# Eleven of 64 pairs of expert units multiplied with seven block products in place of eight, with the block sums made by VectorE

## The reference

```
q = (hb @ w_q) ; s = q . sub_keys ; top-k ; g = softmax(scores of the chosen experts)
act = gelu(einsum('bchkd,bcd->bchk', u[eidx], hb))
...
out = sum over the chosen experts of g * act * v[eidx]
```

## Time and profile before

| | |
|---|---|
| median of 3 timed runs | 2427.67 us (2426.92 to 2431.57) |
| span of the profiled execution, first to last instruction | 2425.6 us |
| TensorE busy | 2404.8 us, 99% |
| VectorE busy | 1756.2 us, 72% |
| ScalarE busy | 1399.6 us, 58% |
| GpSimd busy | 791.8 us, 33% |
| second expert product, layers 0 and 1 | from 867 to 1215 us and from 2073 to 2422 us |

### The profile page before, as it was taken

The page is one execution under the profiler, slowest core; times in us unless marked ns, Lnnn a source line. Parts: engine busy times, 40 slices in busy tenths (PEclk is TensorE's granted clock), DMA queues, the critical chain, the costliest instruction groups (busy, mean ns, idle before and its releaser), DMA issues.

```text
span 2425.6 us, 43553 instructions
## 1 busy us (share of the span) xinstructions
PE 2404.8 (99%) x17531; PEld 2231.4 (92%) x17531; DVE 1756.2 (72%) x2966; ACT 1399.6 (58%) x2071; POOL 791.8 (33%) x452
## 2 busy tenths in 40 slices
PE   9999999999999999999999999999999999999999
PEld 8999999999999988888898999999999999888887
DVE  7988787498489965555678886865974899655555
ACT  5586664444677754445555965644446777544444
POOL 0011410288898820000000113003888998100000
PEclk9999999999999999999999999999999999999999
DMA  6633345355544455566555333453555444555555
GB/s 255 220 122 123 107 144 193 137 186 183 176 163 159 157 187 195 191 215 234 180 191 208 120 126 109 154 186 135 184 183 174 161 162 157 191 191 192 196 194 173
DMA packets 96678, 419.24 MB, mean 173 GB/s; under 512 B 10848, under 2 KB 11360, under 8 KB 79584
## 3 DMA queue, kind: packets, MB, share of 16 engines
q1 hardware_dynamic: 96480, 416.47, 50.5%
HBM read 415.38 MB, written 1.05 MB: 172 GB/s over the span
## 4 chain that ended last, share of the span: by engine, by line
PE 90%; DVE 4%; ACT 2%; DMA 2%; issue 1%; POOL 1%; SPq 0%; DVEq 0%; ACTq 0%
PE banks L2179 28%; PE banks L389 18%; PE banks L391 18%; PE banks L390 18%; PE banks L2161 3%; DMA xr<-in_xstream 1%; PE banks L832 1%; DVE ring_lo L364 1%; PE banks L793 1%; PE banks L809 1%; DMA ring<-in_wstream 1%; POOL xr_lo L1838 1%; PE banks L849 1%; PE banks L2020 0%; PE banks L732 0%
## 5 line engine op out<-in xcount | busy, mean ns | idle before, releaser
L1833 ACT ACTIVATE xr_hi<-xr 128x1024 fp32r<-128x1024 f32 x512 | 541.2, 1058 | 537.1 <-DMA xr<-in_xstream 537.0
L1838 POOL TENSOR_TENSOR xr_lo<-xr,xr_hi 128x1024 fp32r<-128x1024 f32 x256 | 620.1, 2426 | 389.1 <-ACT xr_hi L1833 388.3
L389 PE MATMUL banks<-featH,xr_hi 128*128 128x256 f32 x2048 | 576.7, 282 | 1.8 <-POOL xr_lo L1838 1.8
L390 PE MATMUL banks<-featL,xr_hi 128*128 128x256 f32 x2048 | 575.7, 281 | 0.0
L391 PE MATMUL banks<-featH,xr_lo 128*128 128x256 f32 x2048 | 575.5, 281 | 0.0
L1838 DVE TENSOR_TENSOR xr_lo<-xr,xr_hi 128x1024 fp32r<-128x1024 f32 x256 | 313.8, 1226 | 297.9 <-ACT xr_hi L1833 297.7
L389 PEld LDWEIGHTS banks<-featH,xr_hi 128*128 128x128 f32 x2048 | 386.1, 189 | 2.6 <-POOL xr_lo L1838 1.8
L390 PEld LDWEIGHTS banks<-featL,xr_hi 128*128 128x128 f32 x2048 | 386.4, 189 | 0.0
L391 PEld LDWEIGHTS banks<-featH,xr_lo 128*128 128x128 f32 x2048 | 386.4, 189 | 0.0
L389 PE MATMUL banks<-featH,ring_hi 128*128 128x256 f32 x1232 | 351.8, 286 | 1.2 <-DVE ring_lo L364 0.8
L390 PE MATMUL banks<-featL,ring_hi 128*128 128x256 f32 x1232 | 346.3, 281 | 0.0
(11 more groups left out here) (372 smaller groups left out, 4141.9 us busy)
## 6 DMA issues: line engine op xcount, KB each, us to landing
xr<-in_xstream SPq DMA_DIRECT2D x512, 512.0 KB, 3.3
ring<-in_wstream SPq DMA_DIRECT2D x128, 1024.0 KB, 4.8
smw<-in_small SPq DMA_DIRECT2D x4, 617.0 KB, 10.1
...
big<-in_mix_row SPq DMA_DIRECT2D x4, 256.0 KB, 5.5
```

Source lines behind the costliest of these rows:

```text
L389: PE.matmul(o, s_hi_lo[0], m_hi_lo[0], start=first, stop=False)
L390: PE.matmul(o, s_hi_lo[0], m_hi_lo[1], start=False, stop=False)
L1833: A.activation(xr_hi[:, m % XR], xr[:, m % XR], ACT.Copy).then_inc(s_xhi, 1)
L1838: (PO if m < NKEY else V).tensor_tensor(xr_lo[:, m % XR], xr[:, m % XR], xr_hi[:, m % XR].bitcast(F32), ALU.subtract).then_inc(s_xlo_pool ...
```

## The change

Two units together are a product of a 2x2 block matrix of activations (two token halves by two units) with a 2x2 block matrix of weights (two units by two column halves): eight block products. For the 11 pairs in `SEVEN` the kernel now forms them with Strassen's scheme in Winograd's form: seven block products of four sums of activation blocks and four sums of weight blocks. Each block product has its three passes, so 21 matmuls take the place of 24. Three of the seven go to banks 0 to 2 directly, four gather in banks 4 to 7 over the 11 pairs and are added to x by VectorE at the end (`seven_sums`).

The 22 units of these pairs no longer pass through the ring. `PLAIN` lists the other 106, and `SEVEN_AT` the place in that list ahead of which a pair's seven products stand: 14, 26, 38, 46, then every 6 up to 88. The weights of such a pair come by four transfers of 256 KB (`b_load`) into one of two sets of own buffers: set 0 for pairs 1, 2, 3, 5, 7, 9, 11, set 1 for pairs 4, 6, 8, 10. The memory of set 1 is that of activations which the first 38 units have used up. ScalarE makes the high parts (3584 columns of weights and sums, 1024 of activations and sums), VectorE the sums and the low parts. The positions of these steps in the two engines' loops are tables: for a pair whose products stand ahead of place AT, the steps lie at AT-7 to AT-2, the last of them (`a_low`) at AT-2. The transfers and splits for layer 1's first weights are moved later, since they use buffers that the change needs. Unused semaphores are dropped.

```diff
+SEVEN = (7, 14, 21, 26, 30, 34, 38, 42, 46, 50, 54)
+SEVEN_SET = (0, 0, 0, 1, 0, 1, 0, 1, 0, 1, 0)
+PLAIN = tuple(i for i in range(NKEY) if i // 2 not in SEVEN)
+ONE_BY_ONE = len(PLAIN)
+SEVEN_AT = tuple(2 * r - 2 * j for j, r in enumerate(SEVEN))
...
+                b_sum = [alias(f"b_sum_{i}", [P, 4, 512], F32, offset=sums_at[i]) for i in range(2)]
+                b_sum_lo = [alias(f"b_sum_lo_{i}", [P, 4, 512], F32R, offset=sums_at[i]) for i in range(2)]
...
+                SHARED = tuple(j == 0 or SEVEN_SET[j] == SEVEN_SET[j - 1] or SEVEN_SET[j] not in SEVEN_SET[:j] for j in range(NS))
+                B_HIGH = tuple(SEVEN_AT[j] - 7 if SHARED[j] else SEVEN_AT[j - 1] - 1 for j in range(NS))
...
+                LAST_SUMS = tuple(SEVEN_AT[j] - 6 if SHARED[j] else SEVEN_AT[j - 1] - 1 for j in range(NS))
...
+                A_HIGH = tuple(SEVEN_AT[j] - 5 for j in range(NS))
...
+                SUMS_LOW = tuple(SEVEN_AT[j] - (3 if SHARED[j] else 4) for j in range(NS))
+                A_LOW = tuple(SEVEN_AT[j] - 2 for j in range(NS))
...
+                def load_after(j):
+                    if j == 0:
+                        return 1
+                    if SEVEN_SET[j] not in SEVEN_SET[:j]:
+                        return SEVEN_AT[j - 1]
+                    return max(SEVEN_AT[i] for i in range(j) if SEVEN_SET[i] == SEVEN_SET[j]) + 1
+                def set_free(j):
+                    return j if SHARED[j] and j else max(j - 1, 0)
...
+                    def b_load(j, piece):
+                        sp.wait_ge(s_xu, past(s_xu) + VU + load_after(j) + piece)
+                        if set_free(j):
+                            sp.wait_ge(s_bmul, past(s_bmul) + set_free(j))
+                        unit = VU + 2 * SEVEN[j] + piece // 2
+                        sp.dma_start(b_raw[SEVEN_SET[j]][:, piece],
+                                     xstream[layer * (2 * NKEY) + unit, :, 512 * (piece % 2):512 * (piece % 2 + 1)]
+                                     ).then_inc(s_bl[SEVEN_SET[j]], 16)
...
+                    def seven(j):
+                        b, unit = SEVEN_SET[j], 2 * SEVEN[j]
+                        q, c = unit // QUARTER, unit % QUARTER
+                        a = [(a_hi[b][:, 2 * n + t, :], acts_lo[q][:, c + n, t * P:(t + 1) * P]) for n, t in ((0, 0), (1, 0), (1, 1))]
+                        sums = [(a_sum_hi[b][:, n, :], a_sum_lo[b][:, n, :]) for n in range(4)]
+                        w11, w21, w22 = [(b_hi[b][:, n, :], b_lo[b][:, at, :]) for n, at in enumerate((0, 2, 3))]
+                        t1, t3, t2, t4 = [(b_hi[b][:, 3 + n, :], b_sum_lo[b][:, n, :]) for n in range(4)]
+                        pe.wait_ge(s_bmade, past(s_bmade) + 3 * j + 3)
+                        for p, w, o in ((a[0], w11, 4), (a[1], w21, 0), (sums[3], w22, 1), (a[2], t4, 2),
+                                        (sums[0], t1, 5), (sums[1], t2, 6), (sums[2], t3, 7)):
+                            PE.matmul(bank[o][:], p[0], w[0], start=o >= 4 and j == 0, stop=False)
+                            PE.matmul(bank[o][:], p[0], w[1], start=False, stop=False)
+                            mm = PE.matmul(bank[o][:], p[1], w[0], start=False, stop=o >= 4 and j == NS - 1)
+                        mm.then_inc(s_bmul, 1)
...
-                    for i in range(NKEY - TAIL, NKEY):
+                    for i in range(ONE_BY_ONE - TAIL, ONE_BY_ONE):
                         mm = value(i, 0)
                     mm.then_inc(s_vsum, 1)
-                    for i in range(NKEY - TAIL, NKEY):
...
+                    def b_high(j):
+                        b = SEVEN_SET[j]
+                        act.wait_ge(s_bl[b], past(s_bl[b]) + 64 * (SEVEN_SET[:j].count(b) + 1))
+                        A.activation(b_hi[b][:, 0, :], b_raw[b][:, 0, :], ACT.Copy)
+                        A.activation(b_hi[b][:, 1:3, :], b_raw[b][:, 2:4, :], ACT.Copy).then_inc(s_bhi, 1)
+                    def sums_high(j):
+                        b = SEVEN_SET[j]
+                        act.wait_ge(s_bmade, past(s_bmade) + 3 * j + 1)
+                        A.activation(b_hi[b][:, 3:7, :], b_sum[b][:], ACT.Copy).then_inc(s_bhi, 1)
+                    def a_high(j):
+                        if j == 0:
+                            act.wait_ge(s_xu, past(s_xu) + VU + 6)
+                        b, unit = SEVEN_SET[j], 2 * SEVEN[j]
+                        A.activation(a_hi[b][:].rearrange("p (i t) s -> p i (t s)", i=2), acts[:, unit:unit + 2, :], ACT.Copy
+                                     ).then_inc(s_bhi, 1)
+                    def a_sums_high(j):
+                        b = SEVEN_SET[j]
+                        act.wait_ge(s_bmade, past(s_bmade) + 3 * j + 2)
+                        A.activation(a_sum_hi[b][:], a_sum[b][:], ACT.Copy).then_inc(s_bhi, 1)
 
                     act.wait_ge(s_gev, past(s_gev) + GT)
...
+                        for j in range(NS):
+                            if i == B_HIGH[j]:
+                                b_high(j)
+                            if i == SUMS_HIGH[j]:
+                                sums_high(j)
+                            if i == A_HIGH[j]:
+                                a_high(j)
+                            if i == A_SUMS_HIGH[j]:
+                                a_sums_high(j)
...
+                    def first_sums(j):
+                        b = SEVEN_SET[j]
+                        w = b_raw[b]
+                        dve.wait_ge(s_bl[b], past(s_bl[b]) + 64 * (SEVEN_SET[:j].count(b) + 1))
+                        dch.link(V.tensor_tensor(b_sum[b][:, 0:2, :], w[:, 1:4:2, :], w[:, 0:2, :], ALU.subtract))
+                    def last_sums(j):
+                        b = SEVEN_SET[j]
+                        w, t = b_raw[b], b_sum[b]
+                        dch.link(V.tensor_tensor(t[:, 2, :], w[:, 3, :], t[:, 0, :], ALU.subtract))
+                        V.tensor_tensor(t[:, 3, :], w[:, 2, :], t[:, 2, :], ALU.subtract).then_inc(s_bmade, 1)
+                    def b_low(j):
+                        b = SEVEN_SET[j]
+                        dve.wait_ge(s_bhi, past(s_bhi) + 4 * j + 1)
+                        dve.wait_ge(s_bmade, past(s_bmade) + 3 * j + 1)
+                        V.tensor_tensor(b_lo[b][:, 0, :], b_raw[b][:, 0, :], b_hi[b][:, 0, :].bitcast(F32), ALU.subtract)
+                        V.tensor_tensor(b_lo[b][:, 2:4, :], b_raw[b][:, 2:4, :], b_hi[b][:, 1:3, :].bitcast(F32), ALU.subtract)
+                    def a_sums(j):
+                        b, unit = SEVEN_SET[j], 2 * SEVEN[j]
+                        if j == 0:
+                            dve.wait_ge(s_xu, past(s_xu) + VU + 6)
+                        a11, a21, a12, a22 = [acts[:, unit + n, t * P:(t + 1) * P] for n in range(2) for t in range(2)]
+                        s1, s2, s3, s4 = [a_sum[b][:, n, :] for n in range(4)]
+                        dch.add(V.tensor_tensor(s1, a21, a22, ALU.add))
+                        dch.link(V.tensor_tensor(s3, a11, a21, ALU.subtract))
+                        dch.link(V.tensor_tensor(s2, s1, a11, ALU.subtract))
+                        V.tensor_tensor(s4, a12, s2, ALU.subtract).then_inc(s_bmade, 1)
+                    def sums_low(j):
+                        b = SEVEN_SET[j]
+                        dve.wait_ge(s_bhi, past(s_bhi) + 4 * j + 2)
+                        V.tensor_tensor(b_sum_lo[b][:], b_sum[b][:], b_hi[b][:, 3:7, :].bitcast(F32), ALU.subtract)
+                    def a_low(j):
+                        b, unit = SEVEN_SET[j], 2 * SEVEN[j]
+                        q, c = unit // QUARTER, unit % QUARTER
+                        dve.wait_ge(s_bhi, past(s_bhi) + 4 * j + 4)
+                        dve.wait_ge(s_bmade, past(s_bmade) + 3 * j + 2)
+                        V.tensor_tensor(acts_lo[q][:, c:c + 2, :], acts[:, unit:unit + 2, :],
+                                        a_hi[b][:].rearrange("p (i t) s -> p i (t s)", i=2).bitcast(F32), ALU.subtract)
+                        V.tensor_tensor(a_sum_lo[b][:], a_sum[b][:], a_sum_hi[b][:].bitcast(F32), ALU.subtract).then_inc(s_bmade, 1)
...
+                    def seven_sums(step):
+                        p1, p5, p6, p7 = (bank[n][:] for n in range(4, 8))
+                        if step == 0:
+                            dve.wait_ge(s_bmul, past(s_bmul) + NS)
+                            dch.add(V.tensor_tensor(x_part(0, 0), x_part(0, 0), p1, ALU.add))
+                            dch.link(V.tensor_tensor(x_part(0, 1), x_part(0, 1), p1, ALU.add))
...
+                            if i == A_SUMS[j]:
+                                a_sums(j)
+                            if i == SUMS_LOW[j]:
+                                sums_low(j)
+                            if i == A_LOW[j]:
+                                a_low(j)
+                        if i > SEVEN_AT[NS - 1]:
+                            seven_sums(i - SEVEN_AT[NS - 1] - 1)
```

146 lines of the change are left out of this document (104 added, 42 removed).

## The result

The changed kernel takes 2512.15 us (median of four runs, 2505.07 to 2517.14) against 2428.44 for the kernel before on the same chip: 1.034 times as long, with an interval of 1.0328 to 1.0354. It is slower, as forecast, but by 84 us and not by the 53 of the prediction; it lies 2 us above the top of the range. The profiled run took 2510.55, its span is 2508.7 and its mean granted clock 0.988, where the one before had a span of 2425.6.

What follows compares the result with a forecast made beforehand. TensorE, 90% of the span, was taken as the bound, its feeders only 2.4 us ahead. Per layer 11.6+15.6+5.3+0.8+1.1 = 34.4 us of waits less 7.5 saved, twice: +53.8 on 2425.6, median 2481 us, range 2452 to 2510.

Steps and rivals of the forecast that it cites:

- The mechanism of the waits: Ahead of each pair's seven products: `a_low` behind the ring's low part makes TensorE wait 1.66 us, against 0.68 saved.
- spaced pairs: The 7 pairs per layer standing six places apart: 1.66 us of wait each, 11.6 us per layer.
- The first four pairs: VectorE's and ScalarE's queue ahead of them delays TensorE 3.9 us per pair, 15.6 us per layer.
- the walk: Step-by-step timing of VectorE and ScalarE from unit AT-7 to the products: TensorE starts at 22.9 where 19.04 was due.
- Unit 42: The fourth pair's last piece, landing at T+4.0, makes this unit start 4.3 us late; 5.3 per layer with the queue.
- the queue that starts again: After unit 42's late start: 1.0 us added per layer.
- The later transfers: Transfers for layer 1, some 30 us or more ahead of use: nothing, or up to 2 us if that cover is gone.
- The rest: Per layer, 0.8 us for the adds of `seven_sums` and 1.1 for ring transfers landing later beside the pieces.
- The pace: The 21 matmuls of a pair keep their pace, 4.76 us per pair; another pace got no chance of its own.
- The clock falls: Rival: the new waits of 3 to 4 us could each halve TensorE's clock, up to +17, 2498 us; chance 0.18.
- Only the last wait is real: Rival: VectorE and ScalarE absorb the early sums, 22 waits of 1.66 us stay: +28.9, 2457 us; chance 0.15.
- faster: Rival: the pieces are ready in time and the 15 us saved stay: 2413 us; chance 0.05.

Runs made afterwards that it cites:

- e2: Changed kernel with each pair's seven products one unit later in TensorE's order, other engines' order kept: 2446.39 us, ratio 1.0076.
- e8: Changed kernel with `a_low` one step earlier, at AT-3, ahead of the ring's low part: 2448.43 us, ratio 1.0077.
- e3: Changed kernel with the fourth pair's weight pieces issued two at a time, in two steps instead of four: 2498.23 us, ratio 1.0295.
- e6: Changed kernel with transfers for layer 1 at three places of SyncE's queue moved one unit later: 2505.01 us, ratio 1.0299.
- e5: Changed kernel: products one unit later, fourth and following pairs two pairs later, first four's early steps earlier, layer 1's transfers and splits later: 2419.63 us.

## Why the prediction failed, step by step

- **The mechanism of the waits was right.** `a_low` behind the ring's low part costs more than a pair saves. The delay ahead of the spaced pairs was put at 1.66; in 11 of the 14 it is 1.61 to 1.90 (1.45 to 1.74 of idle time). e2 and e8 remove it from two sides.
- **The first four pairs** were put at 3.9 us each. They wait 2.63 to 3.08 us of idle time; as delays against the pace over the seven units ahead the first three lose 3.54, 4.42 and 3.63 us in layer 0 and 3.59, 3.78 and 3.65 in layer 1, 3.8 on average, so the walk held there. The fourth pair loses only 3.05 and 2.79: the walk didn't reckon with unit 42's wait, which comes four units ahead of it. In all the term was 2.7 us too long. Its price for a 128-wide operation, 0.3, was right: 0.28 to 0.29.
- **Unit 42** was put at 4.3, plus 1.0 for the queue that starts again; it waits 5.31 and 5.11, a delay of 5.5 and 5.3. e3 confirms the cause, the last piece's late landing. The size is luck: in layer 0 the piece landed 5.2 us after T of unit 41 (issued at 1010.91, landed 4.61 us later) and not 4.0, and this 1.2 us, not the queue, filled the 1.0 that was added.
- **The later transfers** were put at nothing, with up to 2 us if their cover was gone. Pairs 7, 8 and 11 of layer 0 wait 6.7 us longer than 1.66 each (1.8, 3.4 and 1.5). At pairs 7 and 8 it is because transfers for layer 1 stand just ahead of the ring transfer that `a_low` waits behind, and e6 shows it; at pair 11 it is argued from the chain alone. That they come 30 us before their use said nothing about whom they delay.
- **The rest** (adds, landing beside pieces) was put at 3.8 us in both layers. Apart from those above I find 1.5 us in waits (0.59, 0.20, 0.41, 0.31) and 1.0 in small losses. These misses nearly cancel, 69.3 us of delay where 68.8 were forecast: that the sum of the waits is so close is luck.
- **The pace** was taken as 4.76 us per pair, with no chance for another. It is 4.86 in the 14 pairs of set 0, 1.4 us in all.
- **The failed step** is "The clock falls". The sum charged nothing for it; it stood as a rival at a chance of 0.18, at 17 us. It came behind every one of the twelve long waits and cost 29.4. The argument against it, that the clock is 1.00 in both stretches, was drawn from a kernel in which no wait there was over 0.4 us; that was no evidence about waits of 3 us. The forecast itself contained ten waits of 3 to 4 us, and the earlier trace rows showed half speed behind 1.9 us. Waits and the clock were one case and not two. The size was too small because its 1.7 us per wait came from one stretch of 3.4 us at half speed and from ten waits; here there are twelve, and behind five of them half speed lasted 6.8 us, as behind the 2.89 us wait, until 1041.5. With 29.4 for the clock the forecast would have been 2510. No forecast could count on all twelve, since in e3 and e6 four waits of 3.06 and 3.08 us had no half speed behind them. The Trainium skill (TensorE: Matmul & The Clock Gate, HAM oscillation) describes the pattern, a long idle gap in each tile of work and a cold start behind it, and proposes a loop order without the gap; the twelve waits agree with the first, and e5, which is at 1.00 in both products, with the second.
- "Only the last wait is real" (2457) is refuted by the first four pairs' waits, nearly twice the size of the spaced ones, "faster" (2413) by 22 waits in 22 pairs.
